# Two transformer blocks on one core: the modulation vector as rows of a 20 by 512 product, scaled by ScalarE

## The reference, cut to what matters

```
gate, up = split(rmsnorm(h) @ w_in);  h = h + 0.5 * (silu(gate) * up) @ w_out      # both feed-forwards, width 2816
c_act = silu(c)                                   # 1 x 1024
mod   = c_act @ w_ada + b_ada                     # 1024 x 6144 weights, 24 MB in all
shift1, scale1, gate1, shift2, scale2, gate2 = split(mod, 6)
h = rms_norm(x, g_pre_mix) * (1.0 + scale1) + shift1
```

## Time and profile before

| | us |
|---|---|
| median of 3 runs | 1005.16 |
| profiled execution, its time | 1004.26 |
| its span | 1002.4 |
| PE busy | 975.8 (97%) |
| DVE busy | 779.9 (78%) |
| ACT busy | 501.8 (50%) |
| POOL busy | 511.0 (51%) |

### The profile page before, as it was taken

The page is one execution under the profiler, slowest core; times in us unless marked ns, Lnnn a source line. Parts: engine busy times, 40 slices in busy tenths (PEclk is TensorE's granted clock), DMA queues, the critical chain, the costliest instruction groups (busy, mean ns, idle before and its releaser), DMA issues.

```text
span 1002.4 us, 18812 instructions
## 1 busy us (share of the span) xinstructions
PE 975.8 (97%) x7645; PEld 926.8 (92%) x7645; DVE 779.9 (78%) x810; ACT 501.8 (50%) x587; POOL 511.0 (51%) x302
## 2 busy tenths in 40 slices
PE   9999999999989999999999999999989989999997
PEld 8999999998979899999999999978979979999996
DVE  5776565799995679887787779998978887768764
ACT  7433433477541474434334756667657454343432
POOL 4575767610054037577577699999940104314400
PEclk9999999999998999999999999999989999999999
DMA  8966858747360277686776475572236517675641
GB/s 270 360 211 227 275 194 276 242 129 211 96 198 8 84 224 244 232 270 209 261 241 213 140 194 159 142 216 85 85 109 204 193 50 245 228 247 195 216 161 43
DMA packets 166494, 190.06 MB, mean 190 GB/s; under 512 B 10654, under 2 KB 155628, under 8 KB 166316
## 3 DMA queue, kind: packets, MB, share of 16 engines
q1 hardware_dynamic: 165580, 186.13, 57.1%
q0 software_dynamic: 688, 3.07, 1.1%
q10 hardware_dynamic: 176, 0.15, 0.1%
HBM read 187.17 MB, written 2.16 MB: 189 GB/s over the span
## 4 chain that ended last, share of the span: by engine, by line
PE 73%; DVE 15%; POOL 4%; issue 3%; ACT 2%; SPq 1%; DMA 1%; ACTq 0%; DVEq 0%; POOLq 0%
PE ps L2079 46%; PE ps L2123 11%; PE ps L2131 9%; DVE wl L1348 5%; DVE ps L1756 2%; POOL work L825 2%; POOL con L822 2%; PE ps L2364 1%; PE ps L2310 1%; ACT wh L856 1%; PE ps L2175 1%; SPq L564 1%; POOL work L818 1%; PE ps L2151 1%; PE ps L2235 1%
## 5 line engine op out<-in xcount | busy, mean ns | idle before, releaser
L2079 PE MATMUL ps<-xh,wh 128*128 128x256 f32 x1208 | 340.1, 282 | 6.4 <-DVE work L1375 3.2
L2079 PE MATMUL ps<-xl,wh 128*128 128x256 f32 x1208 | 335.4, 278 | 0.0
L2079 PE MATMUL ps<-xh,wl 128*128 128x256 f32 x1208 | 335.2, 278 | 0.0
L1353 DVE TENSOR_TENSOR wl<-raw,wh 128x2048 fp32r<-128x2048 f32 x78 | 231.5, 2968 | 67.4 <-ACT wh L862 67.1
L2079 PEld LDWEIGHTS ps<-xh,wh 128*128 128x128 f32 x1208 | 228.1, 189 | 12.3 <-issue 7.1
L2079 PEld LDWEIGHTS ps<-xl,wh 128*128 128x128 f32 x1208 | 227.8, 189 | 0.5
L2079 PEld LDWEIGHTS ps<-xh,wl 128*128 128x128 f32 x1208 | 227.5, 188 | 0.0
L862 ACT ACTIVATE wh<-raw 128x2048 fp32r<-128x2048 f32 x78 | 149.9, 1922 | 138.3 <-PE ps L2079 101.4
L1348 DVE TENSOR_TENSOR wl<-raw,wh 128x2048 fp32r<-128x2048 f32 (+1 forms) x72 | 181.5, 2527 | 32.7 <-ACT wh L856 32.0
L692 POOL TENSOR_TENSOR ada_raw<-ada_raw,c_act 128x2048 f32<-128x2048 f32 x24 | 90.6, 3775 | 206.5 <-DMA ada_raw<-in_w_ada 201.3
L856 ACT ACTIVATE wh<-raw 128x2048 fp32r<-128x2048 f32 (+1 forms) x74 | 139.5, 1889 | 59.4 <-PE ps L2079 42.3
(11 more groups left out here) (426 smaller groups left out, 1773.0 us busy)
## 6 DMA issues: line engine op xcount, KB each, us to landing
raw<-in_ffn_w_in SPq DMA_DIRECT2D x43, 1024.0 KB, 7.6
ada_raw<-in_w_ada SPq DMA_DIRECT2D x24, 1024.0 KB, 5.1
raw<-in_ffn_w_out SPq DMA_DIRECT2D x22, 1024.0 KB, 6.5
raw<-in_w_in SPq DMA_DIRECT2D x18, 1024.0 KB, 5.3
raw<-in_w_mlp_in SPq DMA_DIRECT2D x16, 1024.0 KB, 5.5
raw<-in_w_mlp_out SPq DMA_DIRECT2D x16, 1024.0 KB, 4.9
raw<-in_w_mix_in SPq DMA_DIRECT2D x14, 1024.0 KB, 5.4
raw<-in_w_mix_out SPq DMA_DIRECT2D x4, 1024.0 KB, 5.2
```

The costliest lines, as they stand in the source:

```text
L1353: dve.tensor_tensor(wl[:, s % SLOTS, :], raw[:, s % SLOTS, :], wh[:, s % SLOTS, :].bitcast(F32), ALU.subtract).then_inc(low_done, 1)
L2079: mm = pe.matmul(bank[:, m * T:(m + 1) * T], w[:, k, m * P:(m + 1) * P], r[:, k, :], start=(m == 0 and k == 0 and j == 0), stop=(k == KT - ...
```

## The change: what it does

1. **Steps as rows.** The 20 early steps no longer end in two one-column products. POOL folds `ada_raw` into a buffer of its own (`ada_fold`, 1024, 512, 256 elements), so `ada_raw` is free after the first addition, and SP waits for that only. ACT copies the 256 sums to fp32r (`high_sum`), POOL subtracts to get the low part. PE then makes one fp32r product per pass, 20 by 512 columns, that adds high and low part as row `step` of `ps[7]`, picked by a column of a one-hot line that ACT copies too (`step_pick`).
2. **ACT scales.** From the third step of each feed-forward on, the multiplication by `c_act` is eight ACT copies of 256 elements (`scale_rows`) at the end of ACT's loop iteration. The first two steps are still multiplied by POOL.
3. **PE's pass** ends in that product. The two one-column products, the wait on the gate bank there and `long_zeros` go.
4. **The turn.** In ffn2's last down slab, after half of it, PE turns the 20 rows into columns with four small fp32 products (`turn_rows`), after DVE has copied the rows out of PSUM; DVE adds the bias only after that.
5. **Ahead of slab two** of the mixer and of ffn2 stands a product of 20 by 512 columns (`few_rows`) that the slab overwrites; in ffn1 `long_zeros(ps[7])`, which also clears the bank for the rows.
6. POOL's padding memset of `qkvp` moves behind the ffn1 loop. The four late steps are as before.

```diff
+        ada_fold = {"ffn1": at_mat, "ffn2": w_v[:, 0:1024]}
+        ada_parts = {"ffn1": yl[:, 0:2, :], "ffn2": xh[:, 4:6, :]}
...
 SP  -  modulation(step):
-                if not isinstance(step, int) or step:
+                if late:
                     sp.wait_ge(*at("ada_free", step))
+                elif not isinstance(step, int) or step:
+                    sp.wait_ge(*at("ada_part", step * 5 - 3))
                 sp.dma_start(ada_raw[:, :, :], ...)
...
 POOL
+            def modulation(step, name, scale=True):
+                if scale:
+                    pool.wait_ge(*at("ada_loaded", step * 16 + 16))
+                    pool.tensor_tensor(ada_raw, ada_raw, c_act..., ALU.mult).then_inc(S("ada_part"), 1)
+                else:
+                    pool.wait_ge(*at("ada_free", step))
+                pool.wait_ge(*at("ada_part", step * 5 + 1))
+                pool.tensor_tensor(fold[:, :], flat[:, 0:1024], flat[:, 1024:2048], ALU.add).then_inc(S("ada_part"), 1)
+                ... (512 and 256 elements)
+                pool.wait_ge(*at("ada_part", step * 5 + 5))
+                pool.tensor_tensor(parts[:, 1, :], fold[:, 0:256], parts[:, 0, :].bitcast(F32), ALU.subtract)\
+                    .then_inc(S("ada_free"), 1)
...
 ACT (in ffn)
+                def high_sum(step):
+                    if not isinstance(step, int) or step:
+                        act.wait_ge(*at("ada_taken", step))
+                    act.wait_ge(*at("ada_part", step * 5 + 4))
+                    act.activation(step_pick[:, :], step_line[...], ACT.Copy)
+                    act.activation(ada_parts[name][:, 0, :], ada_fold[name][:, 0:256], ACT.Copy).then_inc(S("ada_part"), 1)
+                def scale_rows(step):
+                    act.wait_ge(*at("ada_loaded", step * 16 + 16))
+                    for k in range(KT):
+                        ins = act.activation(ada_raw[:, k, :], ada_raw[:, k, :], ACT.Copy, scale=c_act[:, k:k + 1])
+                    ins.then_inc(S("ada_part"), 1)
...
                     round_hidden(i + 2)
+                    high_sum(i + (first + 1))
                     cast_in_loop(s + 5, i, 3, 1)
+                with act.Fori(0, FF_STEPS - 3) as i:
+                    one_pass(i)
+                    scale_rows(i + (first + 2))
+                one_pass(FF_STEPS - 3)
...
 PE
+            def few_rows(bank, x):
+                pe.matmul(bank[0:ADA_EARLY, :], x[:, 0, 0:ADA_EARLY], x[:, 0:2, :]..., start=True, stop=True)
+            def modulate(step, name):
+                pe.wait_ge(*at("ada_free", step + 1))
+                pe.matmul(ps[7][0:ADA_EARLY, :], step_pick[:, :], ada_parts[name]..., start=False, stop=False)\
+                    .then_inc(S("ada_taken"), 1)
...
-                    modulate(i + (0 if name == "ffn1" else FF_STEPS - 1))
-                    pe.wait_ge(*at(name + "_gate", i + 2))
-                    long_zeros(gate_bank)
+                    modulate(i + (0 if name == "ffn1" else FF_STEPS - 1), name)
...
+                    if name == "ffn2" and m == 3:
+                        turn_rows()
```

More of the change, by code:

```diff
@@ L663, in _ @@
                     deep(s + 1 + i * 6, s + 1, "w_mlp_out_2", i * 3 + r)
-                modulation(i + ADA_EARLY)
+                modulation(i + ADA_EARLY, late=True)
             for k in range(ADA_MLP * SLOTS + 1, MLP_STEPS):
@@ L684, in _, with modulation_late @@
             pool.memset(zero[:, :], 0.0).then_inc(S("zero"), 1)
-            pool.memset(qkvp[:, :, 0:3], 0.0).then_inc(S("pads"), 1)
+            ps_(pool.memset(step_line[:, :], 0.0))
+            ps_.sync()
+            pool.memset(step_line[:, ADA_EARLY - 1:ADA_EARLY], 1.0).then_inc(S("pads"), 1)
             pool.memset(mpad[:, :, 0:2], 0.0).then_inc(S("pads"), 1)
-            def modulation(step):
+            def modulation(step, name, scale=True):
+                flat = ada_raw[:, :, :].rearrange("p k m -> p (k m)")
+                fold, parts = ada_fold[name], ada_parts[name]
+                if scale:
+                    pool.wait_ge(*at("ada_loaded", step * 16 + 16))
+                    pool.tensor_tensor(ada_raw[:, :, :], ada_raw[:, :, :], c_act[:, :].unsqueeze(2).to_broadcast([P, KT, 256]),
+                                       ALU.mult).then_inc(S("ada_part"), 1)
+                else:
+                    pool.wait_ge(*at("ada_free", step))
+                pool.wait_ge(*at("ada_part", step * 5 + 1))
+                pool.tensor_tensor(fold[:, :], flat[:, 0:1024], flat[:, 1024:2048], ALU.add).then_inc(S("ada_part"), 1)
+                pool.wait_ge(*at("ada_part", step * 5 + 2))
+                pool.tensor_tensor(fold[:, 0:512], fold[:, 0:512], fold[:, 512:1024], ALU.add).then_inc(S("ada_part"), 1)
+                pool.wait_ge(*at("ada_part", step * 5 + 3))
+                pool.tensor_tensor(fold[:, 0:256], fold[:, 0:256], fold[:, 256:512], ALU.add).then_inc(S("ada_part"), 1)
+                pool.wait_ge(*at("ada_part", step * 5 + 5))
+                pool.tensor_tensor(parts[:, 1, :], fold[:, 0:256], parts[:, 0, :].bitcast(F32), ALU.subtract)\
+                    .then_inc(S("ada_free"), 1)
+            def modulation_late(step):
                 flat = ada_raw[:, :, :].rearrange("p k m -> p (k m)")
@@ L716, in _ @@
             pool.wait_ge(low_done, 3)
-            modulation(0)
+            modulation(0, "ffn1")
             pool.dma_start(con[:, N_CONST_FIRST:N_CONST], a["table"][:, N_CONST_FIRST:]).then_inc(S("con_rest"), 16)
@@ L721, in _ @@
             pool.dma_start(t_whole, tiles(dt_mat, UNITS)).then_inc(S("t_blank"), 16)
-            with pool.Fori(0, FF_STEPS - 2) as i:
-                modulation(i + 1)
+            modulation(1, "ffn1")
+            with pool.Fori(0, FF_STEPS - 3) as i:
+                modulation(i + 2, "ffn1", scale=False)
+            pool.wait_ge(*at("ada_taken", FF_STEPS - 1))
+            pool.memset(qkvp[:, :, 0:3], 0.0).then_inc(S("pads"), 1)
             def add_pairs(n, ready, src, pairs=range(4)):
@@ L783, in _ @@
             pool.memset(upad[:, :, 0:PAD], 0.0).then_inc(S("upads"), 1)
-            with pool.Fori(0, FF_STEPS - 1) as i:
-                modulation(i + (FF_STEPS - 1))
+            for i in range(2):
+                modulation(i + (FF_STEPS - 1), "ffn2")
+            with pool.Fori(0, FF_STEPS - 3) as i:
+                modulation(i + (FF_STEPS + 1), "ffn2", scale=False)
+            pool.wait_ge(*at("ada_free", ADA_EARLY))
             pool.wait_ge(*at("pos_loaded", 16))
@@ L840, in _ @@
             with pool.Fori(0, ADA_MLP) as i:
-                modulation(i + ADA_EARLY)
+                modulation_late(i + ADA_EARLY)
         @block.scalar
@@ L895, in round_hidden @@
                     act.activation(high[:, :, :], pair(hid[:, 3, :]), ACT.Copy).then_inc(S(name + "_fh"), 1)
+                def high_sum(step):
+                    if not isinstance(step, int) or step:
+                        act.wait_ge(*at("ada_taken", step))
+                    act.wait_ge(*at("ada_part", step * 5 + 4))
+                    act.activation(step_pick[:, :], step_line[:, bass.ds(step * -1 + (ADA_EARLY - 1), ADA_EARLY)], ACT.Copy)
+                    act.activation(ada_parts[name][:, 0, :], ada_fold[name][:, 0:256], ACT.Copy).then_inc(S("ada_part"), 1)
[4 more added lines that the diff above has]
+                    ins.then_inc(S("ada_part"), 1)
+                first = 0 if name == "ffn1" else FF_STEPS - 1
                 cast(s0 + 3)
@@ L900, in ffn, with one_pass @@
                 round_hidden(1)
-                with act.Fori(0, FF_STEPS - 2) as i:
+                high_sum(first)
+                def one_pass(i):
                     s = s0 + 2
@@ L2151, in long_zeros @@
                 pe.matmul(bank[:, :], zero[0:1, 0:P], zero[0:1, :], start=True, stop=True, skip_group_check=True)
+            def few_rows(bank, x):
+                pe.matmul(bank[0:ADA_EARLY, :], x[:, 0, 0:ADA_EARLY], x[:, 0:2, :].rearrange("p a t -> p (a t)"),
+                          start=True, stop=True, skip_group_check=True)
             def column_sums(n, src, k_tiles, out, ready, signal=True, by_pair=False):
@@ L2183, in square_sums, with turn_rows @@
                 mm.then_inc(S(n + "_stat"), 1)
+            def turn_rows():
+                pe.wait_ge(*at("ada_rows", 1))
+                for half in range(2):
+                    for part in range(2):
+                        mm = pe.matmul(ps[7][:, half * ADA_EARLY:(half + 1) * ADA_EARLY],
+                                       ada_rows[:, part * T + half * P:part * T + (half + 1) * P], ident[0:ADA_EARLY, 0:ADA_EARLY],
+                                       start=(half == 0 and part == 0), stop=(part == 1), skip_group_check=True)
+                mm.then_inc(S("ada_cols"), 1)
             def ffn(name, n, high, low, prev_free):
```

35 lines of the change are left out of this document (23 added, 12 removed).

## The result

The kernel after took 1155.11 us, the median of 4 runs (1149.28 to 1158.65), against 1005.18 before (4 runs, 1004.38 to 1011.98): a ratio of 1.1472, with a 95% interval of 1.1413 to 1.153. It is slower by 150 us. The profiled execution has 1155.57 as its time and 1153.5 as its span, at a mean granted clock of 0.929.

What follows compares the result with a forecast made beforehand. PE's stream bounded the kernel before; after, ACT's wait for the modulation load would: 1004.3 + 75.6 (ffn1) + 74.1 (ffn2) - 0.9 (mixer) + 1.5 (turn) = 1154.6, predicted as 1155 us, range 1095 to 1180.

Steps and rivals of the forecast that it cites:

- The ring: Passes 2 to 9 of each feed-forward: ACT waits for a load its own cast must release; 26.3 us a turn.
- The lock between DVE and POOL: Inside each feed-forward turn: DVE and POOL exclude each other for whole instructions, adding 1.8 us of waiting.
- Where it starts: ffn1's pass 2 starts at 74.9, its last down slab at 275.6; ffn2's pass 2 starts at 422.4.
- PE's own stream: Feed-forward passes: three fast slabs plus 0.27 for the row product, 16.6 us; PE waits some 9.7 a pass.
- rival C: Feed-forwards: the clock stays low for whole passes after PE idles, making PE the bound again; 1231 us, chance 5%.
- The mixer: Five mixer slabs at 5.44 plus 0.4 for the product ahead: 0.9 us gained, or 0.3 lost if the pace stays.
- The turn: End of ffn2: DVE's first bank addition comes 2.4 us late, about 1 is won back; +1.5, between 0.6 and 2.4.
- A: Feed-forwards: the modulation's load lands before ACT comes to its scaling, so nothing waits; 991.6 us, chance 6%.
- rival B: Feed-forwards: load in time, but the 20-column product doesn't set the pace; 17.25 a pass, 1004.8 us, chance 4%.

Runs made afterwards that it cites:

- Experiments 4: Kernel after the change, but ACT scales only one of eight row groups in each early step from the third on: 1109.28 us, ratio 1.1027.
- 5: Kernel after the change, but each modulation load from the second of a feed-forward on brings four of eight row groups: 1128.98 us, ratio 1.1219.
- 6: Kernel after the change, but POOL's three folds of every step that ACT scales take 32, 16 and 8 elements: 1130.67 us, ratio 1.1254.
- experiment 1: Kernel after the change, but the modulation's load stands first in SP's loop iteration instead of last: 995.84 us, ratio 0.99.
- experiment 7: The kernel of experiment 1 run again unchanged, on another chip: 999.5 us, ratio 0.994.
- experiment 3: Kernel after the change, but POOL multiplies in every step and ACT scales nothing: 1080.68 us, ratio 1.0752.
- 9: Kernel of experiment 1, but ACT's `high_sum` stands behind the down slab's cast: 997.5 us, ratio 0.9928.
- experiment 8: Kernel of experiment 1 without the 20 by 512 product ahead of slab two of the mixer and of ffn2: 997.5 us, ratio 0.9917.

## Why the prediction held, step by step

The mechanism is the one forecast: the load that cannot be out, ACT waiting for it ahead of the casts, and the same sixteen rings. That 1155.11 lies within 0.2 of 1155 is luck all the same, since errors of up to 4.4 us cancel, as the third point shows.

- **The ring, 26.3 forecast, 25.67 measured.** By its terms: rounding 0.54, as said; `high_sum` 0.42 instead of 0.7, since the two copies overlap (158.57 to 158.99); the down slab's cast 1.9; its rest and the issue 2.5; the two loads 7.93 instead of 8.2; scaling 3.2 instead of 3.4; the gate slab's cast 1.9. From there to the rounding it is 7.26 instead of 7.1, the lock included; the up values out of PSUM, 0.60 of it (179.13 to 179.73), were missing in the sum. ACT's wait was 10.4 where I had written eight or so: it starts when the cast ends, so by my own terms it was 2.5 + 8.2. Experiments 4, 5 and 6 each took one term down: the ring fell by 2.8, 1.5 and 1.4, and the total by 46, 26 and 24 us. Not all of that is the rings: in experiment 5, for one, pass 2 of ffn1 started 4.3 sooner, as POOL had step 1's load earlier.
- **The lock between DVE and POOL,** 1.8 forecast as two waits (0.5 and 1.3). It came as three longer DVE instructions: 0.45 on the rest of the gate slab, until POOL's first fold ends (174.71 + 2.35 = 177.06); 0.48 on that of the up slab, behind the second fold (to 180.34); 0.53 on the hidden product, behind the third (to 183.08), which I had left out. POOL was held in turn: its second fold took 3.21, and 1.29 where DVE was idle. Each of the five ends about as long after the end of the one before, on the other engine, as it takes alone, less some 0.14: the up slab's rest 2.15 behind the second fold, for one, and 2.28 alone. The Trainium skill (SBUF — State Buffer, "SBUF: two separate sides"), by which the two take turns for whole instructions, agrees with these ends. The second fold lay partly beside DVE's work on the up values, which is why its 1.3 did not count in full. Experiment 6 shows that the folds cause these 1.46.
- **Where it starts.** Pass 2 of ffn1 at 76.64 against 74.9, and the last down slab at 275.48 against 275.6. Three errors cancel there: the start was 1.7 late, as POOL had step 1's load at 47.66 and not at the 45.37 of before; seven rings were 7 x 0.63 = 4.4 short; and the last pass took 19.2 instead of 16.6, as its first products ran at half pace. In ffn2 the last down slab came at 696.55, +147.6 against +148.8, by the same three errors: 1.4 late, 4.1 short, 1.5 long.
- **PE's own stream.** The row product costs 0.23 from start to start, not 0.27, and a pass without waits 16.57 against 16.6 (experiment 1). In the rings the wait was 6.0 to 7.6 (8.6 and 8.4 ahead of pass 2), not 9.7, and 110 in all where I had said about 150: the start of each pass ran at a granted clock of 0.50 (1.2 GHz), all 5.41 of the window above that starts at 204.89, so the first two slabs took 12.4 to 13.7 where 10.9 is full pace. PE had room for that in 25.67, which is why rival C did not come: the clock dipped, and no ring turned slower for it. The fast pace came too, but the row product doesn't set it (last section); as the forecast said, under the ring it doesn't matter.
- **The mixer,** a gain of 0.9 forecast: 27.30 and 0.42 for the product, against 28.55, is 0.8. The stretch between the feed-forwards as a whole gained 0.3.
- **The turn,** +1.5 forecast, +1.95 measured: 14.60 from the last slab's start (696.55) to the second block's first (711.15), against 12.65 (548.96 to 561.61). DVE at the end of ffn2 after:

```profile
697.64 0.67 DVE L1441 COPY work<-ps 20x512 f32<-20x512 f32 x1
700.48 0.20 DVE L1449 TENSOR_TENSOR ada<-ps,vec 128x40 f32<-128x40 f32 x1 [2.16 <-PE ps L2264]
...
701.14 1.29 DVE L1519 SCALAR_TENSOR_TENSOR resid<-ps,resid 128x512 f32<-128x512 f32 x2
```

  The first bank is added 4.6 after the slab's start instead of 1.75; I had 4.1. Of these 2.8, 0.9 is won back, as forecast.
- **Rivals A and B.** Neither came, and A is what experiment 1 made: the load out in time. I had put that at 991.6 for the profiled execution; it took 994.84 in experiment 1 (median 995.84) and 998.9 in experiment 7 (999.5). The 3.2 of experiment 1 are mostly these: passes 1 to 9 of ffn1 took 153.20 and not 149.4, by their first pass, and began 0.7 later; the turn cost 0.9 more than forecast; the stretch between the feed-forwards cost 1.9 less.

PE's row products in ffn1 alternate, 24.8 and 26.4 apart, while the starts of the passes stay 25.6 to 25.8 apart: what alternates is how long PE stays at half pace behind its wait, about 4 and 5.5, and the ring covers that. Still open are the last 1.8 us behind ffn2, within the scatter of the runs.

## What to carry to other kernels

Before work is given to an engine with idle time, ask what it waits for and what stands behind it in that engine's queue, and follow the load it needs back through the queue that issues it: if that issue needs something the same engine still has to release, each iteration pays the whole way round. A wait of an engine that nobody waits for (POOL's 5.3 a step) turns into the bound when its work moves to an engine that feeds the others, and the repair was one line's place in the issuing queue. And a trial that puts only the obvious part back (experiment 3) can meet a second door for the same wait.

## What the runs showed of the hardware that was not expected

PE's 256-column fp32r products, each with its own 128x128 weight load, have two paces at the same granted clock of 1.00: about 113.3 and 117.8 ns from start to start. A pace mostly lasts over slabs without idle time between them. Slab one of pass 1 in ffn1, behind the same row product, first in the kernel after, at the slow pace:

```profile
43.65:49.30 5.65, 5.65 (x49) 1.00 1.01 371
```

then in experiment 1, at the fast one:

```profile
43.67:49.10 5.43, 5.43 (x49) 1.00 0.37 139
```

The row product kept the pace that was on: in ffn1, slow stayed slow behind it in all three profiles in which pass 0 had been slow (the kernel after, experiments 7 and 9), and fast stayed fast in the other eight. In ffn2 it did not always: in experiment 9 three passes behind it took 17.29, 17.19 and 17.19, slow, and the next, behind the same product and with no idle time between, 16.56. So rival B's slow pass exists, and the row product fixes neither pace. The product ahead of the mixer's slab two stood before the fast pace in eight profiles and before the slow one in two (experiments 5 and 7); without it, as before and in experiment 8, the pace was slow. The same instructions are fast in one run and slow in another, so something beyond the program sets it; what isn't settled. The transfers beside it don't decide: pass 2 of ffn2 took 17.19 in experiment 9 at 284 GB/s and 16.57 in experiment 1 at 282. It is worth 0.22 a slab, and 1.05 in the mixer's five.
